# The first half of the fifth tile's output projection in one piece, ahead of the turning of the latent router probabilities

## The reference

```python
m, sf, sb = _mixer(h, ...)            # ends in concat([y_a, y_b]) @ w_out
x = x + gate1 * m
h = _rmsnorm(x, g_norm2) * (1.0 + scale2) + shift2
x = x + gate2 * _ec_moe(h, ...)

def _ec_moe(h, w_router, w_gate, w_up, w_down):
    probs = jax.nn.softmax((h @ w_router).astype(jnp.float32), axis=-1)
    gates, idx = lax.top_k(jnp.swapaxes(probs, 1, 2), cap)   # each expert picks its tokens
    xs = h[bidx, idx]
    a = silu(xs @ w_gate) * (xs @ w_up)                      # per expert
    y = (a @ w_down) * gates
```

## Time and profile before

| | |
|---|---|
| median of 3 runs | 869.84 us (869.76 to 872.36) |
| the profiled execution | 870.74 us, span 869.0 us |
| TensorE busy | 835.3 us, 96% of the span |
| VectorE busy | 492.3 us, 57% |
| ScalarE busy | 236.8 us, 27% |
| GpSimd busy | 63.6 us, 7% |
| moved by DMA | 272.39 MB, mean 313 GB/s |
| granted TensorE clock, mean | 0.992 of full speed |

### The profile page before, as it was taken

The page is one execution under the profiler, slowest core; times in us unless marked ns, Lnnn a source line. Parts: engine busy times, 40 slices in busy tenths (PEclk is TensorE's granted clock), DMA queues, the critical chain, the costliest instruction groups (busy, mean ns, idle before and its releaser), DMA issues.

```text
span 869.0 us, 14535 instructions
## 1 busy us (share of the span) xinstructions
PE 835.3 (96%) x6053; PEld 460.2 (53%) x6053; DVE 492.3 (57%) x1193; ACT 236.8 (27%) x465; POOL 63.6 (7%) x72
## 2 busy tenths in 40 slices
PE   6999999999999999899999999999999999998994
PEld 5798899899998875333333333333333323333322
DVE  3576553858375574676465565664654644654535
ACT  6557643553352325021011011011011011011014
POOL 1000000000000012111011011001001101000023
PEclk9999999999999999999999999999999999999997
DMA  9955715442338758999999999999999999999993
GB/s 330 293 201 189 247 55 184 171 134 97 109 123 356 273 201 328 345 385 420 391 386 412 404 390 409 401 388 397 416 385 387 425 384 401 410 384 409 430 349 140
DMA packets 50325, 272.39 MB, mean 313 GB/s; under 512 B 5226, under 2 KB 14542, under 8 KB 38100
## 3 DMA queue, kind: packets, MB, share of 16 engines
q1 hardware_dynamic: 45340, 255.15, 74.7%
q0 software_dynamic: 3248, 10.88, 5.0%
q10 hardware_dynamic: 1672, 5.43, 1.6%
HBM read 257.95 MB, written 13.57 MB: 312 GB/s over the span
## 4 chain that ended last, share of the span: by engine, by line
PE 80%; DMA 12%; DVE 4%; issue 1%; ACT 1%; SPq 1%; POOLq 0%; POOL 0%; DVEq 0%
PE pair L2349 20%; PE pair L1964 17%; PE pair L2375 11%; PE pair L2326 11%; DMA ring<-in_w_up 10%; PE pair L2384 5%; PE pair L2202 5%; PE pair L1904 2%; PE pair L1999 2%; DMA scale_b<-in_w_mod 2%; DMA xs<-hn,first_ctx 1%; PE pair L2122 1%; PE pair L2134 1%; PE pair L2112 1%; PE pair L2130 1%
## 5 line engine op out<-in xcount | busy, mean ns | idle before, releaser
L2349 PE MATMUL pair<-ring,xT 128*64 128x512 f32 x1024 | 226.7, 598 | 7.5 <-DMA ring<-in_w_up 7.1
L2349 PEld LDWEIGHTS pair<-ring,xT 128*64 128x64 f32 x1024 | 73.8, 137 | 150.1 <-issue 149.5
L2326 PE MATMUL pair<-ring,xT 128*32 128x512 f32 x1024 | 113.4, 594 | 0.9 <-DVE xT L1743 0.9
L2375 PE MATMUL pair<-ring,aT 128*64 128x512 f32 x512 | 113.4, 595 | 0.6 <-DVE aT L1748 0.6
L1131 ACT ACTIVATE xT<-xT,mod,scale 128x64 f32<-128x64 f32 x120 | 41.4, 427 | 217.0 <-DVE xT L1748 217.0
L1748 DVE STREAM_TRANSPOSE xT<-xs 32x256 f32<-32x256 f32 x180 | 78.3, 435 | 3.0
L1748 DVE STREAM_TRANSPOSE aT<-act_l 32x128 f32<-32x128 f32 x256 | 77.5, 303 | 4.1
L2375 PEld LDWEIGHTS pair<-ring,aT 128*64 128x64 f32 x512 | 35.8, 137 | 77.6 <-issue 77.6
L1964 PE MATMUL pair<-hT_hi,w_hi 128*128 128x320 f32 x320 | 75.9, 319 | 0.0
L1782 DVE TENSOR_TENSOR act_l<-act_l,pair 128x512 f32<-128x512 f32 x16 | 11.0, 687 | 113.1 <-ACT act_l L1163 113.1
L2326 PEld LDWEIGHTS pair<-ring,xT 128*32 128x32 f32 x1024 | 31.9, 110 | 80.0 <-issue 80.0
(11 more groups left out here) (304 smaller groups left out, 940.4 us busy)
## 6 DMA issues: line engine op xcount, KB each, us to landing
ring<-in_w_up SPq DMA_DIRECT2D x32, 2048.0 KB, 34.7
ring<-in_w_down SPq DMA_DIRECT2D x32, 2048.0 KB, 25.2
ring<-in_w_gate SPq DMA_DIRECT2D x31, 2048.0 KB, 31.2
p1w<-in_w_mod SPq DMA_DIRECT2D x8, 2048.0 KB, 8.2
p1w<-in_w_in SPq DMA_DIRECT2D x5, 2048.0 KB, 8.1
p1w<-in_w_mod SPq DMA_DIRECT2D x7, 1024.0 KB, 11.2
x_sb<-in_x_sample SPq DMA_DIRECT2D x8, 512.0 KB, 5.8
p1w<-in_w_out SPq DMA_DIRECT2D x2, 2048.0 KB, 8.5
```

Source lines behind the costliest of these rows:

```text
L2326: ins = mm(ctx_ps[32 * g:32 * g + 32, :], xt[:, 4 * half + j, CAP_L:96], w[:, j, n * 512:(n + 1) * 512], start=half == 0 and j == 0, stop= ...
L2349: ins = mm(ps[64 * n:64 * n + 64, :], xt[:, kk, 0:CAP_L], w[:, j, n * 512:(n + 1) * 512], start=kk == 0, stop=kk == KC - 1)
L2375: ins = mm(y_ps[0][r:r + 64, :], aT[:, j, 64 * fh:64 * fh + 64], wd[:, j, n * 512:(n + 1) * 512], start=fh == 0 and j == 0, stop=fh == 1 a ...
```

## The change

TensorE's order is altered in one place. The last three row blocks of tile 4's first half (blocks 5, 6 and 7, nine matmuls of 128x512) stood behind the turned probabilities; they now stand ahead of them.

```diff
             output_projection(4, 0, range(2, 3))
             router_sum(3)
-            output_projection(4, 0, range(3, 5))
+            output_projection(4, 0, range(3, KC))
...
             turn_probs("pT", 1, range(NT - 1))
...
-            output_projection(4, 0, range(5, KC))
             output_projection(4, 1)
```

## The result

The changed kernel takes 871.96 us (median of 22 runs, 869.39 to 873.37). The kernel before, run again beside it, takes 870.32 us (22 runs, 868.51 to 872.36). The ratio is 1.0017 with a 95% interval of 1.0009 to 1.0024: about 1.5 us more. The forecast was 1.0 us more, a time of 870.8 us in a range of 869.0 to 873.0. The executions of either kernel spread over some 4 us, so what follows takes times from medians and mechanisms from the profiled executions. The profiled one took 872.66 us, with a span of 870.9.

What follows compares the result with a forecast made beforehand. The stream of weight loads was taken to bound the expert stage. Load 9's shift of +1.0 us, with nothing behind it given back, was added to the 869.84 us median: 870.8 us, range 869.0 to 873.0.

Steps and rivals of the forecast that it cites:

- The bound: Expert stage: weight-load transfers set the pace, DMA share 1.01 at 399 GB/s, though TensorE looks busy.
- the rule in bold: Before 656 us: a delay of TensorE alone is swallowed by the ring of ten slots; delayed weight loads move the end.
- the cover: At loads 9 and 10: late context rows cost nothing up to 2.7 us, 3.7 with load 9's own lateness.
- The turning and the search: Tile 4's probabilities: turning 1.48 us later, all of it passing through VectorE's search to the indices and gather issue.
- The gather: First expert's gather ahead of load 6: issued 1.48 us later but landing faster, so load 6 at +0.6 us.
- the lower bound: Gather of 64 rows without meeting load 5: 3.4 us, which would leave load 6 at 0.
- the first rival: At load 6: a gather faster by the whole 1.48 us swallows the delay; 869.8 us, down to 868.4; chance 0.12.
- Load 9: Behind tile 4's stores to `sums`: between 0.6 and 1.48 us later, middle taken, +1.0 us.
- The clock's rival: TensorE's wait for indices: its clock falls, adding 0 to 1.7 us; 871.5 to 872.5 us; chance 0.10.
- the forecast's own +0.3 to +2.0 us: Whole kernel: the time rises by this much through the late stream of loads; chance 0.66.
- The store to `hn`: Tile 4, ahead of the context rows: issued at 337.04 us, 11.2 to 14.3 us to landing, context products 1.5 to 4.6 later.
- The rival: Tile 4's store to `hn` falls behind loads 6 and 7, 14.3 us to landing; 874.4 us; chance 0.10.

Runs made afterwards that it cites:

- The two late searches: Search started later, by moving the turning further back on the changed kernel (1.0089) or by 14 extra VectorE maxima on the kernel before (1.0070).
- the late context products: Kernel before with 32 dummy identity products on TensorE ahead of the first expert's context products: 1.0075, median 876.80 us.
- the late load 9: Kernel before with load 9 also waiting until all context products of the first expert are done: 1.0088, median 877.47 us.
- the five executions with the old order: The kernel before, and on it two kernels with dummy products among the context rows (0.9998, 1.0075) and two with load 9 made late (1.0031, 1.0088).
- dummy products over the wait: Changed kernel with 19 instead of 7 dummy identity products ahead of the turned indices: 1.0017, median 872.11 us.
- the kernel with both holes filled: Kernel before with load 6 waiting for GpSimd's root, and tile 4's stores to `sums` right behind ScalarE's copies: 1.0026, median 872.47 us.
- the late turn: Changed kernel with the turning also behind seven of the eight blocks of the second half: 1.0089, median 876.96 us.
- the late search: Kernel before with 14 more maxima ahead of VectorE's search, results unused: 1.0070, median 876.80 us.
- tile 4's early stores: Kernel before with tile 4's two stores to `sums` issued as soon as tile 4 is summed: 0.9995, median 870.03 us.
- the first one with load 9 late: Kernel before with load 9 also waiting for the first half of the first expert's context products: 1.0031, median 873.02 us.
- the kernel with 8 dummy products: Kernel before with 8 dummy identity products on TensorE ahead of the first expert's context products: 0.9998, median 870.22 us.
- the one with load 6 behind the root: Changed kernel with load 6 waiting for GpSimd's root of tile 4 instead of the gather's landing: 0.9997, median 870.88 us.

## Why the prediction was right, step by step

**The bound.** That the stream of weight loads paces the expert stage held. The two late searches, the late context products and the late load 9 all cost time when the DMA engines stood idle, the last with TensorE on time; one more microsecond of TensorE's time cost nothing. But the rule in bold, that a delay of TensorE alone before 656 us is swallowed, was put too widely: TensorE's late context products hold back loads 10 and 11, and 8.7 us of that cost 6.5. It holds up to the cover.

**The turning and the search.** 1.48 us forecast, 1.48 us measured for the turning, and a wait for `selr` of 3.31 us in the forecast range of 3.2 to 3.5. (The restart in the working was 0.09 us, a tenth of a microsecond and not a tenth of the 2.18.) With four times the dose, from TensorE's side or from VectorE's, the cost followed the lateness.

**The gather.** Load 6 at +0.6 us was forecast, +0.65 measured, with the gather at 3.9 us. The value was right, the lower bound under it not: I allowed 3.4 us on idle engines, and it takes 4.0 there. So nearly all that could be saved was saved, not a little over half, and the first rival (the search's delay swallowed whole) could not come true. A row that only the experiments had rules it out. The close agreement is in part luck. In the five executions with the old order the gather took 4.3 to 4.9 us, and load 6 went between 334.76 and 335.35 us, each moved to the place of the one before; in the changed kernel it went at 335.87 on the same scale. So its lateness is 0.5 to 1.1 us, depending on which execution one starts from, and the prediction started from one of the two slowest gathers.

**Load 9.** +1.0 us forecast, +1.21 in the profiled execution (1.08 with the 0.13 taken off), +1.5 in time by the ratio (0.8 to 2.1). If a term was too small, it is this one: I took the middle between load 6's lateness and that of the stores, and it came out near the stores' end. ScalarE issued the stores 2.7 us later than before, not 1.5, because TensorE's lower clock held up tile 4's turned copies in front of them. The forecast of 1.0 us lies inside the interval all the same. Whether the rest of the 1.5 us is this term or the scatter of the last 70 us can't be told apart at this size.

**The clock's rival: its mechanism came true, its price did not show.** I gave it 0.10 as an addition of up to 1.7 us, and two rows that went either way. The clock fell in the profiled execution and made the store to `hn` some 0.9 us later than the 337.04 I had worked out (338.09 less the 0.13). With dummy products over the wait the store came where I had put it (337.02, moved to the same place), and the time was the same. The forecast had it right that the cover takes most of it, but priced the fall itself as unlikely. The absolute time, 871.96 us, even lies in this rival's band (871.5 to 872.5) and not in the forecast's own +0.3 to +2.0 us counted from 869.84. That is because the kernel before, which I took at 869.84 us from three runs, measured 870.32 in twenty-two: by the difference, +1.5 us, it is the forecast that came true.

**The store to `hn`.** 12.2 us to landing, not 14.3. It landed 3.5 us later than before (338.09 + 12.2 against 335.56 + 11.2), and the gather of the context rows was issued at 351.07 us. Two things that I had not reckoned with took up most of these 3.5 us. The gather of the context rows itself had taken 6.0 us and now took at most 3.8, as the rows were there for TensorE at 354.84 us. And TensorE's own chain (tile 4's turning, the dummy products, the first rows at 338.72 and not 336.00 us) was 2.7 us late, so that it no longer had to wait 1.34 us for these rows as before: only its weight load (PEld) still waited 0.81 us for them. So the context products and loads 10 and 11 came 1.31 us later, a little under the 1.5 to 4.6 us that I had given. The rival stayed where it was placed, and the kernel with both holes filled shows that late context rows can cost time.

**The cover.** 3.7 us with load 9's own lateness, 2.7 without. From the one large dose it is 2.2 us, and 0.6 to 3.7 by the interval, so 2.7 is neither confirmed nor refuted; that 1.1 us is covered was seen directly. The 10.2 us in my sum were not those of a load on its own, as the prediction has it, since load 10 went beside it; with 9.4 us the same sum gives 1.9. If the cover was put too large, it had no consequence here: in the changed kernel the share was 0.79 at 356 to 358 us, behind load 9's issue (0.91 before), but 1.01 at 360 to 362, where I had said that it must not fall.

## What to carry to other kernels

In this kernel the time from issue to landing of the weight loads grew from one round to the next while TensorE was busy for 96% of the span, and the doses bear out that the stream was the bound. Where you see this, suspect the stream, test it with a load that is made late, and then ask of an edit only when the stream's next load is issued, and look for the slices in which the DMA share is under 1. A piece of work put ahead of something that an engine already waits for costs its full length less the wait that it fills, here 2.09 less 0.6 us, and an earlier signal is worth nothing if a hole follows behind it (loads 4 and 5 went earlier with the late turn than with the late search, and no gain shows between the two). And read a difference of half a microsecond from more than one profiled execution: the price of the gather that the sum rested on moved by 0.6 us between executions of the same code. The wait worth attacking was the one in front of the hole: a load released by the issue of a small gather and not by its landing gave 2.0 us, but only while another load still bridged the next gap.

## What the runs showed of the hardware

- The gather of 64 rows of 4 KB took 3.9 us in the changed kernel and 4.0 us on idle engines, 4.3 to 4.9 us in five executions of the old order, beside the tail of a 2 MB load, and 6.9 us beside tile 4's early stores. With load 6 issued behind it without waiting for it to land it took 5.6 us on the kernel before and 4.1 us on the changed one.
- The store of 512 KB to `hn` took 10.5 to 12.4 us in every kernel in which load 6 was already out, whether 0.07 or 3.65 us before, and 2.8 us in the one in which it was issued 1.8 us ahead of load 6 (the early stores). Who was issued first went with the time, not by how much. The Trainium skill ("DMA: Bandwidth & Descriptors", "Queues, rings and completion order") has an engine take turns between its queues, a packet at a time. By that alone a load that stands 0.07 us ahead should matter little; these runs don't show what it is that comes first.
- The clock fell to 0.50 after waits of 2.04 and 3.31 us and stayed at 1.00 after one of 3.02 us. The two short waits in front of the context products left it at 1.00 in the kernel before (1.34 and 0.90 us), and it fell behind them in the kernel with the dummy products (0.99 and 0.90 us) and in the first one with load 9 late (1.36 and 0.90 us, 8.60 us for the products). With load 9 later still it stayed at 1.00 behind 1.49 and 0.90 us. In the experts it fell behind a wait of 2.25 us in the kernel with both holes filled (8.78 us for the next 32 products) and stayed at 1.00 behind one of 2.33 us in the kernel with 8 dummy products (7.09 us). And behind the same wait of 3.31 us for the indices it fell within the wait in the changed kernel, but in the one with load 6 behind the root only after tile 4's turning, which still took 1.23 us. The length of a wait does not tell.
- The products with `scale_b`, early in the first phase, which wait for its weights in most executions, start between 23.3 and 24.7 us in fourteen executions of code that is the same up to there. This alone is nearly as much as the change costs.
